# In the delta layer, ScalarE squares the next queries and keys ahead of its copies of the solved values

## The reference

```
qkv, z, a, b = split(rmsnorm(y) @ w_in_c)
q, k, v = split(silu(causal_conv(qkv)))
q, k = l2norm(q) * 128 ** -0.5, l2norm(k)          # 4 heads of 128; v has 8 heads
g, beta = -exp(a_log) * softplus(a + dt_bias), sigmoid(b)
# in chunks, gc = cumsum(g):
m   = strict_lower((k * beta) @ k.T * decay)
u,w = solve(I + m, [v * beta, k * beta * exp(gc)])  # unit triangular
v_new = u - w @ s
o   = (q * exp(gc)) @ s + lower(q @ k.T * decay) @ v_new
s   = s * exp(gc_last) + (k * exp(gc_last - gc)).T @ v_new
y   = y + (rmsnorm(o) * silu(z)) @ w_out_c
```

## Time and profile before

| what | value |
|---|---|
| median of 3 runs | 3452.2 us |
| lowest and highest run | 3446.07 and 3453.64 us |
| profiled execution, first to last instruction | 3455.3 us |
| profiled execution's own time | not given apart from its span |
| mean granted TensorE clock | 0.957 |
| the delta layer in it | about 2780 to 3455 us |
| TensorE busy in the span | 3158.3 us (91%) |
| VectorE, ScalarE, GpSimd busy | 1833.9, 1366.0, 905.2 us |

### The profile page before, as it was taken

How to read it: one execution, slowest core, us unless ns; L and a number is a source line. 1 busy time by engine, 2 the same in 40 slices (tenths; PEclk the granted TensorE clock), 3 DMA queues, 4 the chain that set the end, 5 groups by cost and what they waited for, 6 DMA issues and landing times. The chain is left out here.

```text
span 3455.3 us, 46917 instructions
## 1 busy us (share of the span) xinstructions
PE 3158.3 (91%) x15557; PEld 1730.7 (50%) x15557; DVE 1833.9 (53%) x3700; ACT 1366.0 (40%) x2790; POOL 905.2 (26%) x1776
## 2 busy tenths in 40 slices
PE   8998989989998988888769999999999879989998
PEld 4554444444444444444535444444454456656664
DVE  0000496778878888864221532522514856656663
ACT  2221115667676767676422121121121334433442
POOL 2332333323222221000000000000000567765771
PEclk9999999999999999999879999999999989998999
DMA  6566767555443333300366021111110242234211
GB/s 196 178 197 227 227 209 221 181 163 164 144 130 121 123 111 106 115 28 29 119 217 230 27 68 52 34 64 52 40 61 29 65 161 98 80 98 141 80 62 67
DMA packets 260396, 407.35 MB, mean 118 GB/s; under 512 B 47896, under 2 KB 131138, under 8 KB 258978
## 3 DMA queue, kind: packets, MB, share of 16 engines
q1 hardware_dynamic: 237156, 387.51, 34.6%
q0 software_dynamic: 4096, 8.40, 0.9%
q10 hardware_dynamic: 18912, 8.53, 0.9%
HBM read 324.25 MB, written 103.03 MB: 124 GB/s over the span
## 5 line engine op out<-in xcount | busy, mean ns | idle before, releaser
L2585 PE MATMUL QB<-hT,w_c 128*128 128x512 f32 x1024 | 450.6, 594 | 0.0
L814 PE MATMUL PB<-wb,hT_ahead 128*128 128x512 f32 x832 | 414.5, 625 | 10.6 <-PEq L4174 5.4
L2585 PEld LDWEIGHTS QB<-hT,w_c 128*128 128x128 f32 x1024 | 190.7, 191 | 218.5 <-issue 218.4
L358 PE MATMUL P0A<-w_all,hT 128*128 128x512 f32 (+1 forms) x816 | 268.6, 489 | 2.3 <-issue 2.3
L1007 ACT COPY ptT<-PT 128x512 f32<-128x512 f32 (+3 forms) x320 | 163.8, 518 | 245.1 <-PE PT L825 244.7
L2436 PE MATMUL QA<-arena,hT 128*128 128x512 f32 (+1 forms) x768 | 253.6, 485 | 6.3 <-issue 3.0
L3637 PE MATMUL RPJ<-w_co,oT 128*128 128x512 f32 x544 | 251.7, 612 | 4.2 <-ACT oT L3805 3.2
L963 ACT ACTIVATE signs_out<-isc,mid 128x512 bf16<-128x512 f32 (+6 forms) x168 | 229.5, 1366 | 26.5 <-DVE mid L1107 25.4
L1119 DVE TENSOR_SCALAR_CACHE_REDUCE band<-isc,mid 128x384 bf16<-128x384 f32 (+6 forms) x168 | 236.4, 1407 | 1.3
L814 PEld LDWEIGHTS PB<-wb,hT_ahead 128*128 128x128 f32 x832 | 148.4, 197 | 168.4 <-issue 151.6
L3215 POOL TENSOR_SCALAR stat<-stat 128x1 f32<-128x1 f32 x16 | 3.1, 191 | 816.7 <-POOLq L122 816.7
(11 more groups left out here) (541 smaller groups left out, 5341.7 us busy)
## 6 DMA issues: line engine op xcount, KB each, us to landing
wb<-in_w_in_ab SPq DMA_DIRECT2D x272, 512.0 KB, 3.8
out_c_all<-crow SPq DMA_DIRECT2D x256, 64.0 KB, 1.7
pra<-out_pr_all SPq DMA_DIRECT2D x16, 546.0 KB, 4.7
x_rows<-in_x_all SPq DMA_DIRECT2D x17, 512.0 KB, 5.6
out_hT_all<-hT SPq DMA_DIRECT2D x17, 512.0 KB, 2.9
arena<-out_c_all SPq DMA_DIRECT2D x17, 512.0 KB, 5.0
arena<-out_gc_rows SPq DMA_DIRECT2D x17, 512.0 KB, 3.7
cv<-out_c_all SPq DMA_DIRECT2D x17, 512.0 KB, 5.1
```

The costliest lines, as they stand in the source:

```text
L358: ins = pe.matmul(PA[u % 6][:, 0:b - a], hT[:, t % 3, c, :], w_all[:, c, a:b], start=(c == 0), stop=(c == KD - 1))
L814: ins = pe.matmul(b_bank(g, n)[:, :], h_of(g)[:, 2 * q + k, :], wb[:, u % 4, k, :], start=(q == 0 and k == 0), stop=(q == 3 and k == 1))
L2585: ins = pe.matmul(PB[b % 2][:, 0:N], w_c[:, c, b * P:(b + 1) * P], hT[:, c, 0:N], start=(c == 0), stop=(c == KD - 1))
```

## The change

In ScalarE's list, `qk_squares(t + 3)` moves from behind `level5(t + 1)` to between `blocks(t + 2)` and `solved(t)`. The function itself and the lists of the other engines are unchanged. It moves past `solved`, `query_reads(t, 1)`, `turned_x`, in round 8 the first of `sample_masks`, and `level5`.

```diff
@@ -3845,6 +3845,8 @@
                     sample_query_reads()
                 if live(t + 2):
                     blocks(t + 2)
+                if live(t + 3):
+                    qk_squares(t + 3)
                 if live(t):
                     solved(t)
                 if prompt(t):
@@ -3855,8 +3857,6 @@
                     sample_masks(range(0, 1))
                 if prompt(t + 1):
                     level5(t + 1)
-                if live(t + 3):
-                    qk_squares(t + 3)
                 if live(t + 2):
                     scaled_keys(t + 2)
                 if live(t):
```

## The result

In the first comparison the changed kernel took 3470.75 us at the median of 9 runs (3459.88 to 3476.07), the kernel before 3452.2 us (9 runs, 3446.07 to 3462.49): ratio 1.0051, 95% interval 1.0039 to 1.0063. In a second one it took 3470.56 against 3452.85 us, ratio 1.0050 (1.0036 to 1.0064). The change costs 18.5 us by the medians of the first and 17.7 by those of the second. I had forecast a loss, but 6.9 us, and the result lies above the range, which ended at 3468.

What follows compares the result with a forecast made beforehand. TensorE was taken as busiest, with the squares on its path through L3537. Terms -3.31 (rounds at full clock), -2.0 (round 0), -2.1 (round 8) and +14.3 (clock) gave +6.9 us, 3459.1 us; range 3440 to 3468.

Steps and rivals of the forecast that it cites:

- The wait of 2.2 us: TensorE's wait at L3537 for VectorE's L3936, averaging 2.15 us, was to go entirely, with the falls of clock behind it.
- The loop over L3598, GpSimd, L4010, L3733 and L3755: Path from one round's key products through GpSimd to the next round's, claimed as the next limit at 36.77 us a round.
- Its first half: L3956 to L4010, priced from round 7 at 28.30 us, with L4120 at 1.24 us instead of 0.20.
- the clock: Lower clock over L3628 and L3598 behind TensorE's new gap: 1.3 us in each of 11 rounds, +14.3 us.
- Rounds 3 to 5: Rounds 3 to 6, at 37.55 us before, were to fall to the loop's 36.77: -3.12 us in all.
- its like for rounds 11 to 13: Rounds 11 and 12 at 37.61 us before, with 13, were to fall to the loop's time: 3 x (-0.84) = -2.52 us.
- -3.3: Sum at full clock over rounds 1 to 7 and 9 to 13, without rounds 0 and 8: -3.31 us.
- my -2.1 for round 8: Sample tile's round: squares cost +1.06 us, but L3975 loses some 3.1 us of waiting, so -2.1 us.

Runs made afterwards that it cites:

- `a_busy`: The changed kernel with four useless 128x512 matmuls put into TensorE's idle time ahead of L3628: 3459.11 us, ratio 1.0017 to the kernel before.
- `a_gate`: The changed kernel with VectorE's L3907 moved behind the gating and the add: 3462.13 us, ratio 1.0035 to the kernel before.
- `a_ysq`: The changed kernel with ScalarE's L3733 moved behind the copies L3805: 3419.73 us, ratio 0.9900 to the kernel before; again 3418.88 us, ratio 0.9896.
- `b_third`: The kernel before, unchanged, in a third profile: 542.6 us between first and last L3956, 10.6 us shorter.
- `b_busy`: The kernel before with two useless 128x512 matmuls put into TensorE's gap ahead of L3537: 3453.41 us, ratio 1.0006 to the kernel before.
- `b_ysq`: The kernel before with only ScalarE's L3733 moved behind the copies L3805: 3434.15 us, ratio 0.9933 to the kernel before.
- `b_tail`: The kernel before with one ScalarE copy of one element added behind everything else in the delta layer: its ratio to the kernel before holds 1.
- `b_late`: The kernel before with six small 128x128 TensorE matmuls added ahead of the layer's first L3498: its ratio to the kernel before holds 1.

## Why the prediction was wrong in size, step by step

**Right: what the move does.** The squares sit in ScalarE's idle time, L3891 starts without a wait, L3537 waits no more. The wait of 2.2 us went as worked out, with the falls behind it.

**Right: what is late next.** The loop over L3598, GpSimd, L4010, L3733 and L3755. Its first half measured 28.29 us (28.30 forecast), the whole 36.9 at full clock (36.77), L4120 1.23 us in every round up to 13 but round 8. `a_busy`, `a_gate` and `a_ysq` each took one piece of it away, and the time fell each time, by 11.4, 8.4 and 51 us (15, 11 and 44 expected).

**Right in kind, small in size: the clock.** I had put 1.3 us a round on L3628 and L3598 and measured 1.4: 15.7 and 15.3 us in place of 14.3.

**Wrong: the step "Rounds 3 to 5: (3008.55 - 2895.90)/3 = 37.55; round 6 is alike. 4 x (36.77 - 37.55) = -3.12", and its like for rounds 11 to 13.** I took the rounds of one profile for what the kernel before does, and so credited the change with 0.8 us in each of seven rounds. In its other course five of the seven take 36.0 to 36.2 us, and the change costs 0.7 to 0.9 us in each. The rounds of `a_busy` less those of `b_third` give the same sum at full clock: +1.0 (rounds 1 and 2), +3.3 (3 to 6), +1.6 (9 and 10), +0.7 (11), -1.5 (12 and 13), together +5.2 where I had -3.3. With the clock's 15.7 and round 0's -1.9 (34.10 to 32.23) this makes +19.0, 12.1 us above my 6.9. The course of before is 7.2 of these (its eleven rounds are 406.9 us in the profile I used, 399.7 in `b_third`), the loop at 36.9 is 1.2, the clock 1.4 and round 8 is 2.1. Rounds 7 and 8 together took 108.8 us in `b_third`, 110.0 and 107.6 in the two profiles of the changed kernel; my -2.1 for round 8 can't be told from that scatter. Against the very profile that it was worked from the forecast was about right, with losses in the layer of 8.8 and 6.7 us.

The sign behind that step was in front of me: the loop through L3733 as it stood before is 27.5 + 8.5 = 36.0 us (in the profile before L3956 to L4010 is 27.5 us in rounds 2 to 6), and rounds 1, 9 and 10 took 35.7 to 36.1. Also, the span of that profile, 3455.3 us, lay above the highest of the three timed runs, 3453.64. A kernel held at 36 by one loop cannot go below it by the removal of a wait that another path makes; in `b_busy` the gap at L3537 is almost closed and the rounds stay at 36.0. The change removed the lower of two limits (34.4 against 36.0 us, by `b_ysq`) and lengthened the other by the 1.03 us of L4120 and by the clock.

**Left open.** What decides which course a run of before takes is not shown: two profiles took the long one, three (`b_third`, `b_tail`, `b_late`) the short one, with no difference that I can name between them at the layer's start. That a timed run's clock marks its course is inferred from these five. All ten runs of `b_busy` have 0.962 or more, so by this mark none took the long course, and they still lie 5.5 us above the 14 runs of the upper clock group beside them (medians 3453.4 and 3447.9); why is not shown.

## What to carry to other kernels

When a wait goes, trace what it was waiting beside: take the loop of the next limit from rounds where it stands bare, price it with what runs newly side by side and with the clock over the work behind the new gap, and compare it with the shortest rounds of the kernel before, not with the round on the page. A helper instruction at the head of an in-order list, here the squares of a norm due much later, can be the most expensive one in the kernel: moving L3733 behind four others gained 0.7% by itself and 1.0% together with the change, which alone lost 0.5%. And take more than one profile of the kernel before, and look at whether its timed runs fall into groups by granted clock, before a sum of small differences is built on one.

## What the hardware showed that I had not expected

The same kernel with the same gap of 2.2 us had 0.50 granted for 6.8 us behind it in each of rounds 3 to 6 in one profile, and for 3.4 us in rounds 4 and 6 only in another: 10.6 us between two executions with no difference in work. And matmuls without any use, put into a wait, made the changed kernel 11.4 us faster.
